# The last expert block of a mixture-of-experts layer joined to its tokens by a product with ones

## The reference, cut to what matters

```python
def moe_ffn(h, router_w, router_b, w_in, w_out):
    ...
    gates = jnp.sum(jax.nn.one_hot(expert, N_EXPERTS, dtype=jnp.float32) * top_w[..., None], axis=1).astype(t.dtype)
    y = jnp.zeros_like(t)
    for e in range(N_EXPERTS):
        gu = t @ w_in[e]
        act = jax.nn.silu(gu[:, :D_EXPERT]) * gu[:, D_EXPERT:]
        y = y + gates[:, e:e + 1] * (act @ w_out[e])
    return y.reshape(B, S, D)
```

## Time and profile before

| | us |
|---|---|
| median of 3 runs | 1571.18 |
| lowest, highest | 1570.94, 1571.87 |
| the profiled execution, whole | 1572.3 |
| its span | 1570.5 |
| PE, DVE, ACT, POOL busy in it | 1435.4, 985.6, 776.2, 141.3 |
| its mean granted PE clock | 0.959 |

### The profile page before, as it was taken

One profiled execution on the slowest core, in us unless ns is written; L12 is line 12 of the kernel. 1 busy time (PEld: TensorE's weight loads), 2 busy tenths in 40 slices (PEclk: granted clock), 3 DMA queues, 4 the chain that ended last, 5 costly groups with the idle time before them and its releaser, 6 DMA issues. The chain is left out here.

```text
span 1570.5 us, 19853 instructions
## 1 busy us (share of the span) xinstructions
PE 1435.4 (91%) x7817; PEld 1211.8 (77%) x7817; DVE 985.6 (63%) x1311; ACT 776.2 (49%) x1136; POOL 141.3 (9%) x159
## 2 busy tenths in 40 slices
...
GB/s 192 149 59 110 56 54 55 28 83 133 197 89 81 1 234 192 325 370 378 371 331 200 138 115 81 81 81 73 186 79 56 1 276 230 335 365 380 385 241 213
DMA packets 111006, 274.98 MB, mean 175 GB/s; under 512 B 41777, under 2 KB 44226, under 8 KB 106306
## 3 DMA queue, kind: packets, MB, share of 16 engines
...
## 5 line engine op out<-in xcount | busy, mean ns | idle before, releaser
L185 DVE TENSOR_TENSOR w_lo<-w_stage,w_hi 128x2048 fp32r<-128x2048 f32 (+2 forms) x32 | 67.2, 2104 | 168.3 <-ACT w_hi L175 158.3
L175 ACT ACTIVATE w_hi<-w_stage 128x2048 fp32r<-128x2048 f32 (+2 forms) x34 | 60.2, 1773 | 216.2 <-PE bank L240 113.0
L200 DVE TENSOR_TENSOR w_lo<-w_stage,w_hi 128x2048 fp32r<-128x2048 f32 x42 | 96.2, 2290 | 54.2 <-ACT w_hi L194 29.1
L194 ACT ACTIVATE w_hi<-w_stage 128x2048 fp32r<-128x2048 f32 x40 | 76.5, 1914 | 92.7 <-PE bank L240 55.5
L3002 PE MATMUL bank<-e_wi_lo,e_hx_hi 128*128 128x384 f32 x256 | 86.4, 338 | 0.0
L3001 PE MATMUL bank<-e_wi_lo,e_hx_hi 128*128 128x384 f32 x256 | 86.4, 338 | 0.0
L240 PE MATMUL bank<-w_hi,h_sg_hi 128*128 128x512 f32 x192 | 76.9, 400 | 4.1 <-DVE h_sg_lo L2426 2.1
L2856 DVE TENSOR_TENSOR e_wi_lo<-e_room,w_hi 128x1536 fp32r<-128x1536 f32 x40 | 68.6, 1752 | 13.3 <-ACT w_hi L2852 12.5
L240 PE MATMUL bank<-w_hi,h_sg_lo 128*128 128x512 f32 x192 | 75.7, 394 | 0.0
L240 PE MATMUL bank<-w_lo,h_sg_hi 128*128 128x512 f32 x192 | 75.7, 394 | 0.0
L2860 POOL DMA_INDIRECT e_tok<-moe_h,moe_slots x32 | 64.6, 2020 | 91.3 <-issue 67.1
...
## 6 DMA issues: line engine op xcount, KB each, us to landing
...
```

Source lines behind the costliest of these rows:

```text
L175: act.activation(self.w_hi[h][:, :, :cols], self.stage[h][:, :, :cols], ACT.Copy)\
L185: dve.tensor_tensor(self.w_lo[h][:, :, :cols], self.stage[h][:, :, :cols], self.w_hi[h][:, :, :cols], ALU.subtract).then_inc(self.lo_done[ ...
L194: act.activation(self.w_hi[h][:, :, :cols], self.stage[h][:, :, :cols], ACT.Copy).then_inc(self.hi_done[h], 1)
L200: engine.tensor_tensor(self.w_lo[h][:, :, :cols], self.stage[h][:, :, :cols], self.w_hi[h][:, :, :cols], ALU.subtract).then_inc(self.lo_do ...
```

## The change

The last block is no longer scattered. DVE builds a 128x512 matrix of zeros and ones, `spread` (a row of the block against a token), PE multiplies it by the high and low parts of the block's result (16 products of 128x512), and the result for tile t lies in two banks, to which DVE applies the token's weight in that block (`w_last`, worked out in block 12). The token's ordinary weight for that block is set to zero, so the row read back for it counts nothing; since it is never written, `y_dram` is filled with finite numbers in the attention block. The readback waits for what frees its room and for the scatters before the last. Tiles 0 and 1 add their read rows still within the expert block, tile 2 in the next block on DVE, tile 3 there by ACT (weights) and POOL (sums). `finish(0)` moves between the quarters of the loop's split. Half of the split of the next weight group moves into the next block. The banks of a block's result and of the turned activations change.

```diff
@@ attention block, SP
                 m.load(sp, kv.first + 4)
+                for y in m.y_dram:
+                    for j in range(2 * T):
+                        sp.dma_start(y[j * P:(j + 1) * P, :].rearrange("p (r c) -> p r c", c=P),
+                                     m.ident[:, :].unsqueeze(1).to_broadcast([P, D // P, P])).then_inc(y_filled, 16)
+                sp.wait_ge(y_filled, 16 * 2 * T * DEPTH)
@@ class Combine
+    EARLY = 2
+    BANKS = ((0, 1), (2, 3), (6, 7), (4, 5))
+    def add_row(self, engine, t, c):
+        m, j = self.m, c * T + t
+        engine.wait_ge(m.y_in[j], 16 * (self.layer + 1))
+        return engine.scalar_tensor_tensor(out=m.x[:, t, :], in0=self.y[:, j, :], scalar=m.wgt[:, j:j + 1],
+                                           in1=m.x[:, t, :], op0=ALU.mult, op1=ALU.add)
+    def scale_rows(self, act, t):
+        for c in range(2):
+            j = c * T + t
+            act.wait_ge(self.m.y_in[j], 16 * (self.layer + 1))
+            act.activation(self.y[:, j, :], self.y[:, j, :], ACT.Copy, scale=self.m.wgt[:, j:j + 1]).then_inc(self.scaled, 1)
+    def add_scaled(self, pool, t, past):
+        x = self.m.x[:, t, :]
+        for c in range(2):
+            pool.wait_ge(self.scaled, c + 1)
+            if past + c:
+                pool.wait_ge(self.added[t], past + c)
+            pool.tensor_tensor(x, x, self.y[:, c * T + t, :], ALU.add).then_inc(self.added[t], 1)
     def ready(self, t):
-        return 2 * (t + 1)
+        return 2 if t < self.EARLY else 4
+    def last(self, dve, t, past):
+        m = self.m
+        for n in range(2):
+            if past:
+                dve.wait_ge(self.added[t], past)
+            cols = slice(n * GC, (n + 1) * GC)
+            dve.scalar_tensor_tensor(out=m.x[:, t, cols], in0=m.psum[self.BANKS[t][n]][:, :], scalar=self.w_last[:, t:t + 1],
+                                     in1=m.x[:, t, cols], op0=ALU.mult, op1=ALU.add).then_inc(self.added[t], 1)
@@ moe_experts
+        def rows_free(engine):
+            n = rest(engine)
+            for q in range(CI):
+                engine.wait_ge(w.wi_los[q], n + L)
+            engine.wait_ge(wo_used, L)
+            engine.wait_ge(stored[1], 16 * (NE // 2 - 1))
+            engine.wait_ge(stored[0], n * 16 + 16 * (NE // 2 - 1))
@@ SP, the end
-                sp.wait_ge(stored[1], 16 * (NE // 2))
+                rows_free(sp)
                 combine.load(sp, 0)
@@ POOL, the end
-                scatter(None, 1, ix[:, 1:2])
-                pool.wait_ge(stored[1], 16 * (NE // 2))
+                pool.tensor_copy(last_tok[:, 0:1], slots[:, 0, bass.ds(n + L - 1, 1)]).then_inc(ix_set, 1)
@@ PE, the end
+                pe.wait_ge(spread_made, T)
+                for t in range(T):
+                    for term, (done, part) in enumerate(((last_his, last_hi), (last_los, last_lo))):
+                        for c in range(2):
+                            if t == 0:
+                                pe.wait_ge(done, c + 1)
+                            pe.matmul(m.psum[Combine.BANKS[t][c]][:, :], spread[:, t * P:(t + 1) * P], part[:, c * GC:(c + 1) * GC],
+                                      start=term == 0, stop=term == 1)
@@ ACT, the end
+                rows_free(act)
+                combine.load(act, 1)
                 if upcoming is not None:
                     m.split_hi(act, upcoming)
                 act.wait_ge(wo_used, n + L)
-                finish(1)
-                combine.load(act, 1)
+                for c in range(2):
+                    act.activation(last_hi[:, c * GC:(c + 1) * GC], y_ps[c][:, :], ACT.Copy).then_inc(last_his, 1)
@@ DVE, the end
+                link(dve.tensor_scalar(last_tok[:, :], last_tok[:, :], -float(NO_SLOT), None, ALU.add))
+                link(dve.tensor_tensor(last_at[:, :], last_tok[:, 0:1].to_broadcast([P, T]), rt.codes[:, 0:T, 0], ALU.subtract))
+                for t in range(T):
+                    dve.tensor_scalar(spread[:, t * P:(t + 1) * P], rt.p_row[:, :], last_at[:, t:t + 1], None, ALU.is_equal).then_inc(spread_made, 1)
+                for t in range(Combine.EARLY):
+                    combine.add_row(dve, t, 0).then_inc(early, 1)
+                    dve.wait_ge(early, t + 1)
+                    combine.add_row(dve, t, 1)
                 if upcoming is not None:
-                    m.split_lo(dve, upcoming)
+                    m.half_lo(dve, upcoming, 0)
-                finish(1)
+                for c in range(2):
+                    dve.wait_ge(last_his, c + 1)
+                    dve.tensor_tensor(last_lo[:, c * GC:(c + 1) * GC], y_ps[c][:, :], last_hi[:, c * GC:(c + 1) * GC], ALU.subtract).then_inc(last_los, 1)
@@ sgu_layer, ACT and POOL
+                    combine.add_scaled(pool, T - 1, 2)
...
                         nt.take_root(act, i)
+                        if i == 0:
+                            combine.scale_rows(act, T - 1)
```

106 lines of the change are left out of this document (63 added, 43 removed).

## The result

| | before | after |
|---|---|---|
| median of the runs | 1571.06 us | 1588.97 us (1586.76 to 1590.67) |
| profiled execution: span | 1570.5 us | 1587.8 us |
| mean granted clock | 0.959 | 0.964 |

The changed kernel is slower: the ratio is 1.0113, with a 95% interval of 1.01 to 1.0126, 17.9 us in all. The forecast was 1570.7, within 1566.0 to 1574.0. It missed, and so did all of its rivals. The loss is 1.1% of the time, small but clear of the noise.

What follows compares the result with a forecast made beforehand. The two layers' tails, where the readback needs a scatter of the last block's result, were taken as the target. Layer 1 -2.0, layer 0 +0.5 and +1.0 sum to -0.5 us off the median 1571.18: 1570.7, range 1566.0 to 1574.0.

Steps and rivals of the forecast that it cites:

- Edits priced at nothing: Block 12's weight arithmetic 0 to 0.2 us; later third and fourth quarter's split and exchanged banks without a new wait.
- Layer 1, (1) the copy: Block 14's copy ends at 1531.3, POOL's scatter starts at 1532.15; SP's loads start at 1537, at most 1538.9.
- Layer 1, (2) the rows: ACT issues its loads at 1541.01; tile 0's second row is there 4.43 us later, at 1545.45, further rows in time.
- (3) DVE: Layer 1: three adds end at 1549.4, two low parts at 1550.7; PE waits for these.
- (4) The clock: Layer 1, PE: twelve products remain behind the last low part, 0.23 us each at full clock; barrier at 1554.0.
- a rival that came true: Clock falls in layer 1's product too: nine of twelve products at 0.43 us, 1.8 more, 1572.5; chance 0.10.
- (5) The join behind the block's end: Layer 1: POOL and DVE make each other wait, last half add at 1565.4, store 3.0 us: 2.0 us gained.
- Layer 0, the row: Tile 0's second row there at 848.9, products at the lower clock, square at 863.7: 0.5 us lost.
- ACT's split: Layer 0: placed behind ACT's four loads, ends at 850.5 and is hidden by what follows.
- Tile 1's low part: Layer 0, next stage: ready 17.0 us behind the square against 16.1 before; 1.0 us lost.
- The fill: Attention block: 8.39 MB at 289 GB/s takes 29 us, over at 285; nothing lost.
- that rival: Fill bounds the attention block: at 185 GB/s +10.9 us, 1581.6; decides at about 218 GB/s; chance 0.11.

Runs made afterwards that it cites:

- experiment 2: Kernel before plus only an unused tile of 32 bytes per partition where the change puts its new tile: 1580.57 us, ratio 1.0059.
- experiment 4: Changed kernel with the last weights put into the unused part of the epsilon tile, so no tile moved: 1581.73 us, ratio 1.0065.
- experiment 5: Changed kernel, new tile 64 bytes wide, SP loading both rows of tiles 0 and 1, ACT those of 2 and 3: 1578.07 us, ratio 1.0046.
- experiment 6: Changed kernel, no tile moved, rows dealt to queues by tile, parts PE waits for ahead of the next stage's split: 1569.21 us, ratio 0.999.
- experiment 11: Kernel before plus only the change's sixteen fill transfers (8.39 MB) in the attention block: 1571.69 us, ratio 1.0002.
- experiment 1: Changed kernel with its new tile of last weights made 64 bytes wide per partition: 1584.69 us, ratio 1.0088.
- experiment 7: On top of experiment 6, DVE adds tile 2's two rows inside the block while PE multiplies: 1563.9 us, ratio 0.9949.
- experiment 8: On top of experiment 1, DVE adds tile 3's rows instead of ACT scaling and POOL adding them, both layers: 1583.88 us, ratio 1.0073.
- experiment 9: On top of experiment 7, ACT's scalings and POOL's sums for tile 3 ahead of the block's end in layer 1: 1570.27 us, ratio 0.9992.
- experiment 10: On top of experiment 7, ACT's scalings and POOL's sums for tile 3 ahead of the block's end in both layers: 1575.75 us, ratio 1.0023.
- experiment 3: Kernel before plus only an unused tile of 64 bytes per partition where the change puts its new tile: 1575.64 us, ratio 1.0025.

## Why the forecast was wrong

Every step is compared on the scale of the kernel before, less the lag that PE already had when ACT left the loop (16.03 us in layer 1, 2.63 in layer 0, the lag of the last block's products). Two steps failed: a term that was missing altogether, and the landing of the rows.

- **The step that failed most: a term put at nothing.** "Edits priced at nothing" has the weight arithmetic, the split and the banks, and no term for where operands lie. A new tile of 16 bytes was priced by what is computed in it, never by what it moves. Experiments 2 and 4 put 9.2 and 7.2 us on it, the largest single part of the 17.9, and this alone carries the time out of the stated range.
- **Layer 1, (1) the copy: right, the landing late.** Forecast of the scatter 1532.15, measured 1548.08 less 16.03 = 1532.05. SP's first load stood at 1554.52, so 1538.5 on the old scale, 1.5 later than the value taken and inside its bound of 1538.9.
- **Layer 1, (2) the rows: wrong, the second step that failed.** "In the trace the first row is used 4.43 us behind the first issue" was read where both queues began together and nothing was under way. Tile 0's second row is now ACT's first load, behind four loads of SP's of which three are for later tiles. Issue came 1.1 us later than forecast (1558.15 against 1557.04), and the row 6.2 us behind the issue instead of 4.4: 1564.32 against 1561.5, 2.8 late. DVE used SP's own first row 4.0 us behind its issue and had not waited for it, so the 4.4 was no underestimate for whoever comes first. The forecast asked whether SP's rows would be there, and not what they would do to ACT's.
- **(3) DVE: right in its parts**, 3.80 and 1.28 us, and named as the place where PE would wait. It inherits the 2.8.
- **(4) The clock: a rival that came true.** PE now waited 4.34 us, the granted clock fell to 0.57 between 1568 and 1572, and fourteen products took 5.02 us. The rival's price, 1.8 us, was about right, but its condition was not independent: it hung on step (2). With the rows in time (experiment 5) the granted clock stayed at 1.00 and sixteen products took 4.6.
- **(5) The join behind the block's end: right.** 11.4 us forecast, 10.7 measured (1574.09 to 1584.79), with POOL and DVE in turns as assumed. The store took its 3.0. In sum the last half add came at 1584.79 less 16.03 = 1568.8 instead of 1565.4: 1.2 us lost, where 2.0 were to be gained.
- **Layer 0, the row: wrong by the same step.** 855.38 against 848.9 + 2.6 = 851.5, 3.9 late: ACT's first issue came 1.1 us late again, at 848.17, and the row 7.2 us behind it. The lower level of the clock was the right choice for the first eight products (0.43 us or more from start to start); the last six followed at 0.25 or less, so the mean was 0.37. The square stood at 868.87 less 2.63 = 866.2 against a forecast of 863.7: 3.0 us lost instead of 0.5. ACT's split "is hidden by what follows" was right, since the row was later still; once the row is in time, it and DVE's half split are next (experiment 6: 2.4 us).
- **Tile 1's low part: right.** 17.0 us behind the square forecast, 886.05 less 868.87 = 17.2 measured; before it was 16.1.
- **The fill and the weight arithmetic: right.** The fill ran at 286 to 342 GB/s, above the row of 185 and above the 218 at which it would have mattered; experiment 11 shows no cost. (The price of that rival holds a slip: 301.4 less 290.84 is 10.6, not 10.9.) "0 to 0.2 us" for the weight arithmetic fits the trace, in which PE's lag grows by 0.2 behind block 12 of each layer.
- **Not foreseen and not tested.** At the start of both expert stages PE's clock came up later than before, 0.8 and 1.0 us by the lag. It shows in some of the experiments and not in others, and what sets it is open. And PE's wait for the weights in the second cross attention (experiment 4) stands in the kernel after and all eight changed versions of it, 0.84 to 1.46 us, and in none of the kernel before and its three variants (0.15 or less). In the kernel after it costs 0.7 us. There ACT could start on these weights 7.6 us behind the first issue (1272.12 to 1279.74), in the kernel before 6.7 (1258.81 to 1265.47). It thus comes with the change, in a stage that the change does not touch; why is open.

The lag, taken at the same landmarks in every trace, tells the tails from the rest. In us, with a minus for time gained: up to the last block's products of layer 0, from there to the third group, from there to the last block's products of layer 1, and from there to the end of the span.

| kernel | ahead | layer 0's tail | between | layer 1's tail |
|---|---|---|---|---|
| after | 2.6 | 4.1 | 9.3 | 1.3 |
| experiment 1 (tile of 64 bytes) | 0.3 | 4.1 | 5.9 | 1.0 |
| experiment 4 (no tile moved) | -1.6 | 5.3 | 3.5 | 1.2 |
| experiment 5 (1, and rows by tile) | -0.7 | 1.5 | 6.8 | -4.4 |
| experiment 6 (4, rows, parts first) | -1.9 | -0.8 | 2.7 | -4.4 |
| experiment 7 (6, and tile 2 early) | 1.1 | -2.7 | 2.2 | -7.6 |
| experiment 8 (1, DVE alone) | 1.4 | 3.5 | 5.7 | 2.6 |
| experiment 9 (7, sums early in layer 1) | -0.3 | -2.7 | 1.9 | -2.5 |
| experiment 10 (in both layers) | -1.8 | 4.2 | 2.7 | -3.1 |
| experiment 2 (before, 32 bytes) | 1.4 | 0.4 | 7.1 | 0.0 |
| experiment 3 (before, 64 bytes) | 0.2 | -0.1 | 3.4 | -0.1 |
| experiment 11 (before, the fill) | -2.0 | -0.1 | -0.1 | 0.0 |

Experiment 11 gives PE nothing else to do, and its first column shows by how much an execution can differ early on; its other columns stay within 0.15. These are single traces, so the first column should not be read to better than 2 us.

In the kernel after, of the 9.3 us between the tails 1.0 are the clock's late return, 0.7 the wait for the weights and 0.2 the weight arithmetic; the 7.4 left are about what the placement alone costs there in experiment 2, 7.1. The rows (experiment 5 against 1) are worth 2.6 and 5.5 us in the two tails; the medians say 6.6, since the profiled execution of experiment 5 was the fastest of its five. The order of the parts (6 against 5, ACT's and DVE's list changed together) is worth 2.4 in layer 0 and nothing in layer 1, and tile 2's early adds (7 against 6) 1.9 and 3.2. So 9.2 for the placement (experiment 2), 8.1 for the rows and 2.4 for the order make 19.7, against 19.8 between the changed kernel and experiment 6. That close a match is in part luck, since experiment 4 gave 7.2 and not 9.2 and the clock and the wait for the weights move as well. Experiment 6 is 2.3 us below the kernel before, on the side of the 0.5 that the forecast gave the change, but with two orders that the forecast did not have.

The Trainium skill (SBUF — State Buffer, SBUF: two separate sides) says that DVE and GpSimd lock a shared pair of ports for a whole instruction, and that a DVE instruction with two SBUF inputs takes part in that. The traces agree: 5.29 us for DVE's two adds beside POOL's sums (experiment 1) against 2.60 without them (experiment 8). They also agree in the other direction: DVE's half adds, with one input in a bank, ran at 0.67 us beside POOL's sums in experiment 7 (six in 4.04), and POOL's sums at 2.4 instead of 2.8 each.
